# Two output blocks taken in turn: the order of the matmuls in a three-product fp32r trunk

## The chip, the cores and the metric

The kernel runs on one core of one Trainium2 chip. The metric is the device time of one launch in microseconds (us), median of three runs.

## The reference

The reference is a two-layer post-norm decoder trunk on x of 512 tokens by 1024 features, float32 throughout. Only the parts that matter here:

```
for i in range(2):
    x = layer_norm(ALPHA * x + 0.5 * swiglu(x, ffn1_w_gu[i], ffn1_w_down[i]), ...)
    if i == 0: y, qm = gla_mix(x @ gla_w_in, ...)      # gated linear attention
    else:      y, qm = conv_mix(x @ conv_w_in, ...)    # GLU, 31-tap depthwise convolution, layer norm
    m = mem_attention(qm, mem, mem_w_kv[i])            # 256 memory rows, 4 heads
    x = layer_norm(ALPHA * x + concatenate([y, m]) @ w_out, ...)
    x = layer_norm(ALPHA * x + 0.5 * swiglu(x, ffn2_w_gu[i], ffn2_w_down[i]), ...)

def swiglu(x, w_gu, w_down):                           # w_gu 1024 x 5632, w_down 2816 x 1024
    a, b = split(x @ w_gu, 2); return (silu(a) * b) @ w_down
```

## The kernel before

**Layout.** Activations are kept transposed: features on the 128 partitions, the 512 tokens along the free dimension, so x is eight blocks of 128x512. A PSUM bank holds one output block of 128x512 float32.

**Three products.** Every large product runs in the fp32r form of the matmul. A float32 operand is split into a rounded part (hi) and the remainder (lo), and a product is the sum of hi*hi, hi*lo and lo*hi (weights named first). `mm3` (L1228) issues these three, one after the other, into one bank: L1231 with weights whi and activations hi, L1232 with whi and lo, L1233 with wlo and hi. Every matmul comes with a weight load of its own.

**Weights.** They stream through in 206 chunks of up to eight k-blocks by 256 columns (two output blocks, called t = 0 and 1), in two slots. For each chunk SP loads it into `raw`, ACT rounds it into `whi` (`split_hi`, L479) once the slot is free (`w_used`), POOL (sometimes DVE) subtracts to make `wlo` (`split_lo`, L314, L870) and raises `lo_ready`, for which PE waits. Each engine's order is written out by hand; PE, ACT, DVE and POOL meet in semaphores only.

**The stages around the change.**
- `chunk` (L1235) is one chunk against x: k outside, t inside, so that the bank changes after every three matmuls. Used for the gate/up product of each of the four FFNs (22 chunks each; one bank pair for gate, one for up) and for the input projections. Two chunks of the GLA projection have one output block only, on bank 2 alone (`chunk(n0 + 1, 1, (2,))`, `chunk(n0 + 3, 1, (2,))`, L1485, L1492).
- `by_halves` (L1246) is the form of the first chunk after a layer norm, which follows x block by block as it becomes ready: per k two matmuls into the first bank, two into the second (L1253), then one each of the previous k's lo part (L1258).
- `down_pair` (L1275) is the FFN's second product: four pairs p of output blocks, each over 22 k-blocks in four chunks c of 6, 6, 6 and 4. Inside a chunk t is outside and k inside: all matmuls of t = 0 (bank 0), then all of t = 1 (bank 1). In the last chunk `y_even` is raised after t = 0, `w_used` after t = 1. Pairs 1 to 3 use the same two banks, and wait per bank for its evacuation (`y_evac`). Pairs 1 and 2 are a hardware loop on PE, ACT and DVE.
- `out_a` and `out_b` (L1350, L1362) are the output projections: over four k-blocks of the memory attention and eight of the mixer; t outside, k inside, two bank pairs. On PE the order is out_a(0), out_a(1), out_b(0), out_b(1), out_a(2), out_a(3), out_b(2), out_b(3), with a by_halves in place of out_b(0) after the convolution.
- `shift_sum` (L1299) stands on PE right behind pair 0 of each of these six products. It sums the first finished block over partitions and so waits for the first evacuation of the pair. `sums_u` (L1315) stands before the last k-block of pair 3.

**What follows a pair.** On DVE `residual_pair` (L911) takes, for t = 0: the residual (L923, and L927 in the output projections, L921 for the first block), the wait for `y_even`, the evacuation of bank t = 0 with the add (L934), the running sum (`add_sum`, L895; in pair 0 instead `take_shift`, L909); for t = 1: the running sum of squares of the block before (`add_square`, L903 or L900), the residual, the wait for `w_used`, the evacuation (L934), the sum, the square. On ACT `down_pair` (L514) has the splits of the coming chunks up to c = 0 of the next pair, then `squares` (L508) of both blocks, each after its evacuation, and only then the split of c = 1 of the next pair. In `out_proj` (L525) the split for slot 1 of out_a(3) stands behind the squares of pair 1, and that of the next stage's first chunk behind those of block 4 and 5.

Of the kernel before, what the change touches and what calls it, by code (L numbers as in the profile page):

```python
# [85 lines left out]
def build(nc, a, out):  # L86
    kv_dram = nc.dram_tensor("kv_scratch", (DEPTH, P, 2048), F32, kind="Internal").ap()
    with ExitStack() as ctx:
# [775 lines left out]
        def _(dve):  # L864
# [78 lines left out]
            def residual_ffn(ln, n0):  # L943
                residual_pair(ln, 0, n0 + 4, 0.5)
                with dve.Fori(1, 3) as p:
                    residual_pair(ln, p, n0 + 4 * p + 4, 0.5)
                residual_pair(ln, 3, n0 + 16, 0.5, last=True)
# [279 lines left out]
        def _(pe):  # L1227
# [6 lines left out]

            def chunk(n, s, banks, ready=None):  # L1235

                pe.wait_ge(lo_ready, n + 1)
                if ready is not None:
                    last = by_halves(s, banks, xhi, xlo, ready, True)
                else:  # L1240
                    for k in range(DK):
                        for t, b in enumerate(banks):
                            last = mm3(bank[b][:, :], s, k, t, xhi[:, k, :], xlo[:, k, :], k == 0, k == DK - 1)
                last.then_inc(w_used, 1)

            def by_halves(s, banks, hi, lo, ready, start):  # L1246

                for k in range(DK + 1):
                    if k < DK:
                        pe.wait_ge(x_hi_ready, ready + k + 1)  # L1250
                        for t, b in enumerate(banks):
                            for half in (whi, wlo):
                                nc.tensor.matmul(bank[b][:, :], half[:, s, k, t * P:t * P + P], hi[:, k, 0:SEQ],  # L1253
                                                 start=(start and k == 0 and half is whi), stop=False)
                    if k:
                        pe.wait_ge(x_ready, ready + k)
                        for t, b in enumerate(banks):
                            last = nc.tensor.matmul(bank[b][:, :], whi[:, s, k - 1, t * P:t * P + P], lo[:, k - 1, :],  # L1258
                                                    start=False, stop=(k == DK))
                            if k == DK and t == 0 and not start:  # L1260
                                last.then_inc(y_even, 1)
                return last
# [12 lines left out]
            def down_pair(f, p):  # L1275

                ln, n = LN_FFN[f], FFN_N[f] + FK + 4 * p
                first = isinstance(p, int)
                k0 = 0
                for c, kc in enumerate(DOWN_K):  # L1280
                    pe.wait_ge(lo_ready, n + c + 1)
                    if first and p == 0:
                        pe.wait_ge(h_done, FK * f + k0 + kc)
                        if c == 0:
                            pe.wait_ge(silu_done, FK * (f + 1))
                    for t in range(2):
                        if c == 0 and not (first and p == 0):
                            pe.wait_ge(y_evac, 8 * ln + 2 * p - 1 + t)
                        for k in range(k0, k0 + kc):
                            if first and p == 3 and t == 1 and k == FK - 1:  # L1290
                                sums_u(ln)
                            last = mm3(bank[t][:, :], c % 2, k - k0, t, h_hi[:, k, :], h_lo[:, k, :], k == 0, k == FK - 1)
                        if t == 1:
                            last.then_inc(w_used, 1)
                        elif c == len(DOWN_K) - 1:
                            last.then_inc(y_even, 1)
                    k0 += kc
# [41 lines left out]
            def ffn(f, between=None):  # L1339
# [5 lines left out]
                with pe.Fori(1, 3) as p:  # L1345
                    down_pair(f, p)
                down_pair(f, 3)
                stats(LN_FFN[f], (GLA_N, FFN_N[2], CONV_N, None)[f])

            def out_a(ln, n0, p, m, mo_hi, mo_lo):  # L1350
# [6 lines left out]
                for t in range(2):  # L1357
                    for k in range(A_K):
                        last = mm3(bank[b0 + t][:, :], p % 2, k, t, mo_hi[:, k, :], mo_lo[:, k, :], k == 0, False)
                last.then_inc(w_used, 1)  # L1360

            def out_b(ln, n0, p, y_h, y_l, base):  # L1362
# [3 lines left out]
                if p == 0 and base is not None:  # L1366
                    by_halves(0, (0, 1), y_h, y_l, base, False).then_inc(w_used, 1)
                    return
                for t in range(2):
                    for k in range(B_K):  # L1370
                        if p == 0 and t == 0:
                            pe.wait_ge(y_done, k + 1)
                        if p == 3 and t == 1 and k == B_K - 1:
                            sums_u(ln)
                        last = mm3(bank[b0 + t][:, :], p % 2, k, t, y_h[:, k, :], y_l[:, k, :], False, k == B_K - 1)
# [70 lines left out]
            for n in range(8):  # L1446
# [3 lines left out]
                for k in range(DK):  # L1450
                    if n == 0:
                        pe.wait_ge(mem_ready, k + 1)
                    for t in range(2):
                        last = mm3(bank[2 * (n % 2) + t][:, 0:NMEM], n % 2, k, t, mem_hi[:, k, :], mem_lo[:, k, :], k == 0, k == DK - 1)
# [157 lines left out]
            def diag_chunk(g):  # L1612
# [5 lines left out]
                for j in range(TAPS_K[g]):  # L1618
                    tap = 8 * g + j
                    for t in range(2):  # L1620
                        last = mm3(bank[2 + t][:, :], g % 2, j, t, cin_hi[:, t, tap:tap + SEQ], cin_lo[:, t, tap:tap + SEQ],
                                   tap == 0, tap == WIDTH - 1)
# [81 lines left out]
```

## Time and profile before

| | |
|---|---|
| median of 3 runs | 2279.32 us (2277.9 to 2279.92) |
| profiled execution, first to last instruction (span) | 2278.2 us |
| its mean granted TensorE clock | 0.967 |
| PE busy | 2163.0 us, 95% |
| PEld (weight loads) | 1748.7 us, 77% |
| POOL, DVE, ACT busy | 944.2, 830.9, 697.3 us |
| DMA | 195.62 MB, mean 86 GB/s |

The profiled execution comes with its span alone; no separate time of it is given, and the span is 1.1 us under the median. PE is TensorE's matmuls, PEld its weight loads (they run beside matmuls), DVE VectorE, ACT ScalarE, POOL GpSimd, SP SyncE. The durations of matmuls overlap, as a matmul starts before the one before has drained, so the pace is read from starts. A granted clock of 1.00 is 2.4 GHz, 0.50 is 1.2 GHz.

### The profile page before, as it was taken

The numbers are of one execution on the slowest core, as the hardware profiler recorded it, in microseconds if no ns is written. First come the engines' busy times: TensorE is split into PE (matmuls) and PEld (weight loads), VectorE is DVE, ScalarE is ACT, GpSimd is POOL, SyncE is SP. The second block draws the span as 40 slices with busy tenths as digits, with TensorE's granted clock in tenths as the row PEclk, the third lists the DMA queues.
The fourth block names the chain that finished last, engine by engine and source line by source line (L and its number), as shares of the span: only waits on it lengthen the run. The fifth ranks groups of instructions, "written<-read, shape, count | busy, mean of one in ns | idle before, by whom it ended". The sixth has DMA issues, their size and how long they took to land.

```text
span 2278.2 us, 24232 instructions
## 1 busy us (share of the span) xinstructions
PE 2163.0 (95%) x9608; PEld 1748.7 (77%) x9608; DVE 830.9 (36%) x963; ACT 697.3 (31%) x900; POOL 944.2 (41%) x295
## 2 busy tenths in 40 slices
PE   7999999999899999999999999998587899999998
PEld 7888888678777788887868888776465577888886
DVE  2233221424425432331142332125499753332213
ACT  5322222364313322222232222224145333222222
POOL 3244433443122444443344443436776234444342
PEclk9999999999989999999999999999798799999999
DMA  6422222232102223222322222232110122223221
GB/s 207 166 92 92 94 84 95 70 111 82 48 19 91 76 96 106 92 78 88 111 71 96 92 92 83 89 106 75 56 37 7 49 93 74 92 92 98 83 91 60
DMA packets 191706, 195.62 MB, mean 86 GB/s; under 512 B 3567, under 2 KB 190061, under 8 KB 191388
## 3 DMA queue, kind: packets, MB, share of 16 engines
q1 hardware_dynamic: 191036, 192.62, 26.0%
q10 hardware_dynamic: 608, 2.13, 0.2%
q8 instruction: 44, 0.72, 0.1%
q14 instruction: 18, 0.15, 0.0%
HBM read 190.54 MB, written 4.19 MB: 85 GB/s over the span
## 4 chain that ended last, share of the span: by engine, by line
PE 85%; DVE 5%; POOL 4%; ACT 3%; issue 1%; DMA 1%; DVEq 0%; POOLq 0%; ACTq 0%
PE bank L1231 26%; PE bank L1233 26%; PE bank L1232 26%; POOL wlo L314 3%; PE bank L1306 1%; DVE u L1173 1%; POOL xlo L324 1%; ACT u L543 1%; PE bank L1576 1%; ACT whi L479 1%; DMA raw<-in_mem_w_kv_dram 1%; PE bank L1332 1%; DVE scratch L895 1%; DVE scratch L956 0%; PE bank L1570 0%
## 5 line engine op out<-in xcount | busy, mean ns | idle before, releaser
L314 POOL TENSOR_TENSOR wlo<-raw,whi 128x2048 fp32r<-128x2048 f32 (+2 forms) x184 | 786.6, 4275 | 1155.9 <-ACT whi L479 1155.9
L1231 PE MATMUL bank<-xhi,whi 128*128 128x512 f32 x1712 | 673.4, 393 | 35.9 <-POOL wlo L314 35.9
L479 ACT CAST whi<-raw 128x2048 fp32r<-128x2048 f32 (+2 forms) x202 | 341.5, 1690 | 1194.4 <-PE bank L1233 1157.8
L1233 PE MATMUL bank<-xhi,wlo 128*128 128x512 f32 x1712 | 669.9, 391 | 0.0
L1232 PE MATMUL bank<-xlo,whi 128*128 128x512 f32 x1712 | 669.9, 391 | 0.0
L1231 PEld LDWEIGHTS bank<-xhi,whi 128*128 128x128 f32 x1712 | 323.6, 189 | 105.8 <-issue 37.8
L1233 PEld LDWEIGHTS bank<-xhi,wlo 128*128 128x128 f32 x1712 | 323.3, 189 | 67.7
L1232 PEld LDWEIGHTS bank<-xlo,whi 128*128 128x128 f32 x1712 | 323.7, 189 | 67.3 <-issue 0.5
L877 DVE TENSOR_TENSOR scratch<-scratch,bank 128x512 f32<-128x512 f32 x88 | 56.5, 684 | 631.5 <-PE bank L1233 631.5
L1231 PE MATMUL bank<-h_hi,whi 128*128 128x512 f32 x704 | 281.0, 399 | 0.1
L1233 PE MATMUL bank<-h_hi,wlo 128*128 128x512 f32 x704 | 278.5, 396 | 0.0
L1232 PE MATMUL bank<-h_lo,whi 128*128 128x512 f32 x704 | 278.5, 396 | 0.0
L880 DVE TENSOR_TENSOR h_lo<-scratch,h_hi 128x512 f32 (+1 forms) x88 | 223.3, 2575 | 53.2 <-ACT h_hi L496 53.2
L934 DVE SCALAR_TENSOR_TENSOR u<-bank,u 128x512 f32<-128x512 f32 (+1 forms) x48 | 33.2, 691 | 404.9 <-PE bank L1233 403.4
L1231 PEld LDWEIGHTS bank<-h_hi,whi 128*128 128x128 f32 x704 | 132.5, 188 | 34.7 <-POOL wlo L314 1.9
L1232 PEld LDWEIGHTS bank<-h_lo,whi 128*128 128x128 f32 x704 | 132.5, 188 | 32.0 <-issue 1.0
L1233 PEld LDWEIGHTS bank<-h_hi,wlo 128*128 128x128 f32 x704 | 132.5, 188 | 32.0
L1173 DVE SCALAR_TENSOR_TENSOR u<-conv_in,w_dw,u 128x512 f32<-128x512 f32 x170 | 131.1, 843 | 0.0
L324 POOL TENSOR_TENSOR xlo<-u,xhi 128x512 fp32r<-128x512 f32 x48 | 70.0, 1477 | 48.0 <-ACT u L543 28.9
L508 ACT ACTIVATE scratch<-u 128x512 f32<-128x512 f32 (+1 forms) x56 | 35.1, 632 | 154.0 <-DVE u L934 136.2
L870 DVE TENSOR_TENSOR wlo<-raw,whi 128x2048 fp32r<-128x2048 f32 (+1 forms) x18 | 40.7, 2262 | 58.2 <-ACT whi L479 58.2
L496 ACT CAST h_hi<-scratch 128x512 f32 (+1 forms) x88 | 49.9, 615 | 0.0
(235 smaller groups left out, 1913.8 us busy)
## 6 DMA issues: line engine op xcount, KB each, us to landing
raw<-in_ffn_w_gu_dram SPq DMA_DIRECT2D x88, 1024.0 KB, 5.0
raw<-in_ffn_w_down_dram SPq DMA_DIRECT2D x48, 768.0 KB, 4.4
raw<-in_gla_w_in_dram SPq DMA_DIRECT2D x13, 1024.0 KB, 5.3
raw<-in_conv_w_in_dram SPq DMA_DIRECT2D x10, 1024.0 KB, 5.0
raw<-in_mem_w_kv_dram SPq DMA_DIRECT2D x8, 1024.0 KB, 6.6
raw<-in_ffn_w_down_dram SPq DMA_DIRECT2D x16, 512.0 KB, 3.4
raw<-in_gla_w_out_dram SPq DMA_DIRECT2D x4, 1024.0 KB, 5.2
raw<-in_conv_w_out_dram SPq DMA_DIRECT2D x4, 1024.0 KB, 5.1
```

The costliest lines, as they stand in the source:

```text
L314: nc.gpsimd.tensor_tensor(wlo[:, s, 0:kc, 0:width], raw[:, s, 0:kc, 0:width], whi[:, s, 0:kc, 0:width].bitcast(F32), ALU.subtract).then_in ...
L324: nc.gpsimd.tensor_tensor(lo[:, k, :], u[:, k, :], hi[:, k, 0:SEQ].bitcast(F32), ALU.subtract).then_inc(x_ready, 1)
L479: nc.scalar.copy(whi[:, s, 0:kc, 0:width], raw[:, s, 0:kc, 0:width]).then_inc(hi_ready, 1)
L496: nc.scalar.copy(h_hi[:, bass.ds(2 * i + t, 1), :], act_out[t].rearrange("p (a s) -> p a s", a=1)).then_inc(h_hi_done, 1)
L508: nc.scalar.activation(sq[t], u[:, bass.ds(d, 1), :].rearrange("p a s -> p (a s)"), ACT.Square).then_inc(sq_done, 1)
L870: nc.vector.tensor_tensor(wlo[:, s, 0:kc, 0:width], raw[:, s, 0:kc, 0:width], whi[:, s, 0:kc, 0:width].bitcast(F32), ALU.subtract).then_in ...
L877: nc.vector.tensor_tensor(act_out[t], act_out[t], bank[2 + t][:, :], ALU.mult).then_inc(mul_done, 1)
L880: nc.vector.tensor_tensor(h_lo[:, bass.ds(2 * i + t, 1), :], act_out[t].rearrange("p (a s) -> p a s", a=1), h_hi[:, bass.ds(2 * i + t, 1), ...
L1173: nc.vector.scalar_tensor_tensor(out=u[:, c, :], in0=src, scalar=w, in1=u[:, c, :], op0=ALU.mult, op1=ALU.add).then_inc(taps_done, 1)
L1231: nc.tensor.matmul(to, whi[:, s, k, w], hi, start=start, stop=False)
L1232: nc.tensor.matmul(to, whi[:, s, k, w], lo, start=False, stop=False)
L1233: return nc.tensor.matmul(to, wlo[:, s, k, w], hi, start=False, stop=stop)
```

## The change

Where `mm3` gave all three products of one output block, a new helper gives each product for both blocks before the next product, so that consecutive matmuls write two banks in turn. Chunks, the memory keys' projection, the convolution's taps and the out and down products use it; `by_halves` turns its two inner loops round. The four down pairs use banks 0, 1 and 2, 3 alternately (`b0 = 2 * (p % 2)`), wait for the evacuation of the pair before the last one only, and are unrolled on PE and DVE. In pair 3 the last chunk of `down_pair`, and the last four k-blocks of `out_b`, keep t outside and the order of `mm3`. The number of matmuls and of weight loads is the same.

```diff
 def residual_ffn(ln, n0):
-    residual_pair(ln, 0, n0 + 4, 0.5)
-    with dve.Fori(1, 3) as p:
-        residual_pair(ln, p, n0 + 4 * p + 4, 0.5)
-    residual_pair(ln, 3, n0 + 16, 0.5, last=True)
+    for p in range(4):
+        residual_pair(ln, p, n0 + 4 * p + 4, 0.5, b0=2 * (p % 2), last=p == 3)
...
+def mm3_in_turn(tos, s, k, his, los, start, stop):
+    for n, (half, xs) in enumerate(((whi, his), (whi, los), (wlo, his))):
+        last = [nc.tensor.matmul(to, half[:, s, k, t * P:t * P + P], xs[t], start=(start and n == 0),
+                                 stop=(stop and n == 2)) for t, to in enumerate(tos)]
+    return last
...
 def chunk(n, s, banks, ready=None):
         for k in range(DK):
-            for t, b in enumerate(banks):
-                last = mm3(bank[b][:, :], s, k, t, xhi[:, k, :], xlo[:, k, :], k == 0, k == DK - 1)
+            last = mm3_in_turn([bank[b][:, :] for b in banks], s, k, [xhi[:, k, :]] * 2, [xlo[:, k, :]] * 2,
+                               k == 0, k == DK - 1)[-1]
...
 def by_halves(s, banks, hi, lo, ready, start):
-            for t, b in enumerate(banks):
-                for half in (whi, wlo):
+            for half in (whi, wlo):
+                for t, b in enumerate(banks):
...
 def down_pair(f, p):
-    ln, n = LN_FFN[f], FFN_N[f] + FK + 4 * p
-    first = isinstance(p, int)
+    ln, n, b0 = LN_FFN[f], FFN_N[f] + FK + 4 * p, 2 * (p % 2)
+    to = [bank[b0][:, :], bank[b0 + 1][:, :]]
     for c, kc in enumerate(DOWN_K):
...
-        for t in range(2):
-            if c == 0 and not (first and p == 0):
-                pe.wait_ge(y_evac, 8 * ln + 2 * p - 1 + t)
+        elif p >= 2 and c == 0:
+            pe.wait_ge(y_evac, 8 * ln + 2 * (p - 2) + 2)
+        if p == 3 and c == len(DOWN_K) - 1:
+            for t in range(2):
+                for k in range(k0, k0 + kc):
+                    if t == 1 and k == FK - 1:
+                        sums_u(ln)
+                    last = mm3(to[t], c % 2, k - k0, t, h_hi[:, k, :], h_lo[:, k, :], False, k == FK - 1)
+                last.then_inc(w_used if t else y_even, 1)
+        else:
             for k in range(k0, k0 + kc):
-                if first and p == 3 and t == 1 and k == FK - 1:
-                    sums_u(ln)
-                last = mm3(bank[t][:, :], c % 2, k - k0, t, h_hi[:, k, :], h_lo[:, k, :], k == 0, k == FK - 1)
-            if t == 1:
-                last.then_inc(w_used, 1)
-            elif c == len(DOWN_K) - 1:
-                last.then_inc(y_even, 1)
+                even, last = mm3_in_turn(to, c % 2, k - k0, [h_hi[:, k, :]] * 2, [h_lo[:, k, :]] * 2,
+                                         k == 0, k == FK - 1)
+            if c == len(DOWN_K) - 1:
+                even.then_inc(y_even, 1)
+            last.then_inc(w_used, 1)
...
 def ffn(f, between=None):
-    with pe.Fori(1, 3) as p:
+    for p in range(1, 4):
         down_pair(f, p)
-    down_pair(f, 3)
...
 def out_a(ln, n0, p, m, mo_hi, mo_lo):
-    for t in range(2):
-        for k in range(A_K):
-            last = mm3(bank[b0 + t][:, :], p % 2, k, t, mo_hi[:, k, :], mo_lo[:, k, :], k == 0, False)
+    for k in range(A_K):
+        last = mm3_in_turn([bank[b0][:, :], bank[b0 + 1][:, :]], p % 2, k, [mo_hi[:, k, :]] * 2,
+                           [mo_lo[:, k, :]] * 2, k == 0, False)[-1]
...
 def out_b(ln, n0, p, y_h, y_l, base):
+    to = [bank[b0][:, :], bank[b0 + 1][:, :]]
+    together = B_K - 4 if p == 3 else B_K
+    for k in range(together):
+        if p == 0:
+            pe.wait_ge(y_done, k + 1)
+        even, last = mm3_in_turn(to, p % 2, k, [y_h[:, k, :]] * 2, [y_l[:, k, :]] * 2, False, k == B_K - 1)
+    if p < 3:
+        even.then_inc(y_even, 1)
+        last.then_inc(w_used, 1)
+        return
     for t in range(2):
-        for k in range(B_K):
-            if p == 0 and t == 0:
-                pe.wait_ge(y_done, k + 1)
-            if p == 3 and t == 1 and k == B_K - 1:
+        for k in range(together, B_K):
+            if t == 1 and k == B_K - 1:
                 sums_u(ln)
-            last = mm3(bank[b0 + t][:, :], p % 2, k, t, y_h[:, k, :], y_l[:, k, :], False, k == B_K - 1)
+            last = mm3(to[t], p % 2, k, t, y_h[:, k, :], y_l[:, k, :], False, k == B_K - 1)
         last.then_inc(w_used if t else y_even, 1)
```

The products of the memory keys and of the convolution's taps change in the same way as `out_a`.

## Rows read from the trace of the kernel before

**Rows 1.** The page: the chain that ended last, shares of the span by engine
```profile
PE 85%; DVE 5%; POOL 4%; ACT 3%; issue 1%; DMA 1%; DVEq 0%; POOLq 0%; ACTq 0%
```

**Rows 2.** Windows, PE alone: stretch, its us, PE busy (x matmuls touched), granted clock, DMA
```profile
100.00:300.00 200.00, 200.00 (x884) 1.00 0.29 96
350.00:430.00 80.00, 80.00 (x345) 1.00 0.30 92
```

**Rows 3.** Timeline of PE, one-bank chunk, first and last of 18 (start, duration, us)
```profile
477.29 0.39 PE L1231 MATMUL bank<-xhi,whi 128*128 128x512 f32 x1
...
481.14 0.39 PE L1233 MATMUL bank<-xhi,wlo 128*128 128x512 f32 x1
```

**Rows 4.** Timeline of PE, by_halves of the first FFN: 18 matmuls from first to last start
```profile
69.71 0.39 PE L1253 MATMUL bank<-xhi,whi 128*128 128x512 f32 x1
...
73.79 0.39 PE L1253 MATMUL bank<-xhi,whi 128*128 128x512 f32 x1
```

**Rows 5.** Timeline of PE, first FFN: last even matmul of pair 1, first of pair 2's c = 0 and 1
```profile
368.30 0.40 PE L1233 MATMUL bank<-h_hi,wlo 128*128 128x512 f32 x1
...
371.34 0.40 PE L1231 MATMUL bank<-h_hi,whi 128*128 128x512 f32 x1
...
379.73 0.39 PE L1231 MATMUL bank<-h_hi,whi 128*128 128x512 f32 x1
```

**Rows 6.** Timeline of DVE at that boundary
```profile
368.74 0.69 DVE L934 SCALAR_TENSOR_TENSOR u<-bank,u 128x512 f32 x1 [23.59 <-PE bank L1233]
...
372.96 0.69 DVE L934 SCALAR_TENSOR_TENSOR u<-bank,u 128x512 f32 x1
```

**Rows 7.** Timeline of ACT and of POOL at that boundary
```profile
373.78 0.64 ACT L508 ACTIVATE scratch<-u 128x512 f32 x1 [3.52 <-DVE u L934]
374.32 1.47 ACT L479 CAST whi<-raw 128x1536 fp32r<-128x1536 f32 x1
...
367.57 3.50 POOL L314 TENSOR_TENSOR wlo<-raw,whi 128x1536 fp32r<-128x1536 f32 x1 [6.51 <-ACT whi L479]
375.87 3.50 POOL L314 TENSOR_TENSOR wlo<-raw,whi 128x1536 fp32r<-128x1536 f32 x1 [4.79 <-ACT whi L479]
```

**Rows 8.** Timeline of DVE, GLA output projection, pair 1: the steps without a loop
```profile
729.03 0.69 DVE L895 TENSOR_TENSOR scratch<-scratch,u 128x512 f32<-128x512 f32 x1
729.69 0.69 DVE L903 TENSOR_TENSOR scratch<-scratch 128x512 f32<-128x512 f32 x1
730.30 0.68 DVE L923 SCALAR_TENSOR_TENSOR u<-xlo,scratch 128x512 f32<-128x512 f32 x1
731.02 0.69 DVE L927 SCALAR_TENSOR_TENSOR u<-xhi,u 128x512 f32<-128x512 f32 x1
731.75 0.69 DVE L934 SCALAR_TENSOR_TENSOR u<-bank,u 128x512 f32<-128x512 f32 x1
```

**Rows 9.** Timeline of PE: a shift sum that waited; and a half-clock stretch, its first matmul and the first past it
```profile
1830.83 1.13 PE L1301 MATMUL bank<-u,ones 128*128 128x512 f32 x2 [0.74 <-DVE u L934]
...
1620.64 0.77 PE L1231 MATMUL bank<-xhi,whi 128*128 128x512 f32 x1 [28.63 <-POOL wlo L314]
...
1625.32 0.39 PE L1233 MATMUL bank<-xhi,wlo 128*128 128x512 f32 x1
```

**Rows 10.** Timeline of ACT, POOL and PE, GLA output: out_a(2) to out_a(3)
```profile
733.01 1.04 ACT L479 CAST whi<-raw 128x1024 fp32r<-128x1024 f32 x1
...
734.12 2.39 POOL L314 TENSOR_TENSOR wlo<-raw,whi 128x1024 fp32r<-128x1024 f32 x1 [6.40 <-ACT whi L479]
...
736.61 0.46 PE L1231 MATMUL bank<-mo_hi_g,whi 128*128 128x512 f32 x1
```

**Rows 11.** Timeline of POOL, DVE and PE, GLA output, out_b(3): to sums_u
```profile
756.97 4.65 POOL L314 TENSOR_TENSOR wlo<-raw,whi 128x2048 fp32r<-128x2048 f32 x1 [7.83 <-ACT whi L479]
...
760.07 2.11 DVE L895 TENSOR_TENSOR scratch<-scratch,u 128x512 f32<-128x512 f32 x1
...
763.97 0.50 PE L1306 MATMUL bank<-ones,scratch 128*128 128x1 f32 x4
```

More of the change, by code:

```diff
@@ L1281, in down_pair @@
                     pe.wait_ge(lo_ready, n + c + 1)
-                    if first and p == 0:
+                    if p == 0:
                         pe.wait_ge(h_done, FK * f + k0 + kc)
@@ L1368, in out_b @@
                     return
+                to = [bank[b0][:, :], bank[b0 + 1][:, :]]
+                together = B_K - 4 if p == 3 else B_K
+                for k in range(together):
+                    if p == 0:
+                        pe.wait_ge(y_done, k + 1)
[4 more added lines that the diff above has]
+                    return
                 for t in range(2):
-                    for k in range(B_K):
-                        if p == 0 and t == 0:
-                            pe.wait_ge(y_done, k + 1)
-                        if p == 3 and t == 1 and k == B_K - 1:
+                    for k in range(together, B_K):
+                        if t == 1 and k == B_K - 1:
                             sums_u(ln)
-                        last = mm3(bank[b0 + t][:, :], p % 2, k, t, y_h[:, k, :], y_l[:, k, :], False, k == B_K - 1)
+                        last = mm3(to[t], p % 2, k, t, y_h[:, k, :], y_l[:, k, :], False, k == B_K - 1)
                     last.then_inc(w_used if t else y_even, 1)
@@ L1452, in _ @@
                         pe.wait_ge(mem_ready, k + 1)
-                    for t in range(2):
-                        last = mm3(bank[2 * (n % 2) + t][:, 0:NMEM], n % 2, k, t, mem_hi[:, k, :], mem_lo[:, k, :], k == 0, k == DK - 1)
+                    last = mm3_in_turn([bank[2 * (n % 2) + t][:, 0:NMEM] for t in range(2)], n % 2, k, [mem_hi[:, k, :]] * 2,
+                                       [mem_lo[:, k, :]] * 2, k == 0, k == DK - 1)[-1]
                 last.then_inc(w_used, 1)
@@ L1619, in diag_chunk @@
                     tap = 8 * g + j
-                    for t in range(2):
-                        last = mm3(bank[2 + t][:, :], g % 2, j, t, cin_hi[:, t, tap:tap + SEQ], cin_lo[:, t, tap:tap + SEQ],
-                                   tap == 0, tap == WIDTH - 1)
+                    last = mm3_in_turn([bank[2][:, :], bank[3][:, :]], g % 2, j, [cin_hi[:, t, tap:tap + SEQ] for t in range(2)],
+                                       [cin_lo[:, t, tap:tap + SEQ] for t in range(2)], tap == 0, tap == WIDTH - 1)[-1]
                 last.then_inc(w_used, 1)
```

## The prediction

> **What bounds the kernel now.** The chain that ended last comes first: 85% of the span on PE [rows 1]. So what matters is the pace of PE's matmuls and the places where PE waits. The exception is the convolution, where PE waits for POOL (28.63 us before one matmul [rows 9]) and a faster PE would bring little.
>
> The pace comes from windows. Between 100 and 300 us PE never rests, and 884 matmuls touch the 200 us; less the two at the ends that makes 0.2268 us each. In the down product it is 80 / 343 = 0.2332 us [rows 2]. At the granted clock of 1.00 (2.4 GHz) 512 columns pass in 0.2133 us, so 6% and 9% are lost inside the stream. The change is about that loss, if the loss comes from the bank.
>
> **Does the bank set the pace?** The kernel has three mixtures of bank changes on the same operands. In `chunk` one succession in three changes the bank: 0.2268 us. In the one-bank GLA chunk none does: 18 matmuls, 17 steps in 3.85 us, 0.2265 us [rows 3]. In `by_halves` four of six do, three of them in a row: 18 steps in 4.08 us, 0.2267 us [rows 4]. None, a third and two thirds of changes give the same pace to 0.1%. The slower down product repeats one bank, but so does the one-bank chunk, which is fast; what differs there is the activations (h in place of x), which the change does not move. I therefore take the changes of pace at nothing, for 7,248 matmuls of 512 columns. Bounds: if full alternation does what two thirds do not, each falls to 0.2133 us (the second rival); the products on h could fall to 0.2267, or pick up a further 0.007 us.
>
> The Trainium skill says the same of the mechanism: in "TensorE: Matmul & The Clock Gate", Step-by-step, the next matmul's fill overlaps the drain of the last, with no word of the bank, and its Back-to-back issue gap has 216 ns for 512 columns. The rows are 5 to 8% over that figure with and without a bank change; if the change closed that gap, the result would lie near the second rival's.
>
> **What the rotation of the down pairs saves.** In pairs 1 to 3 PE asks for the evacuation of the bank that it is about to fill. Where pair 2 begins PE goes on without a gap: the 13 steps from 368.30 to 371.34 us take 3.04 us, or 0.234 each [rows 5]. Nothing saved. Unrolling saves nothing either, as these steps go across a turn of the loop.
>
> **What the turn order costs.** In the old order block t = 0 of a pair is done a stretch of matmuls before t = 1: 12 in the FFN, 24 in `out_b`, some 2.8 and 5.6 us. DVE and ACT use them. In turn, t = 0 is done one matmul before t = 1, and their work comes in one piece behind the pair. ACT's order then matters: the split of the next pair's chunk c = 1 is queued behind the squares of both blocks, so behind both evacuations.
>
> *FFN, entry of pairs 2 and 3.* Let E be the start of the next pair, 371.34 [rows 5]. Now the odd evacuation starts at E + 1.62 [rows 6], the square 0.82 later, the split 0.54 later, POOL 1.55 later, for 3.50 [rows 7]: wlo is there at E + 8.03. PE needs it at 379.73 = E + 8.39 [rows 5]. There is only 0.36 us of slack. After the change the even evacuation starts 0.44 after its last matmul starts (368.74 less 368.30) [rows 5, 6], which now is two steps before E: E - 0.03. Then, by the steps of the code without a loop: evacuation to sum 0.73, sum to square's sum 0.66, to residual 0.61, to odd evacuation 0.72 [rows 8]. That is E + 2.69. ACT's square follows one such step later, then 0.54 + 1.55 + 3.50 as before: E + 9.01, and 0.05 to PE. PE waits 0.67 us, and 0.1 us more for the first matmul after a wait. Two entries in four FFNs: 8 x 0.75 = **6.0 us**. With loop steps (0.82 and 0.81) it would be 1.1 each; if a hand-over is hidden, 0.4. Pair 1 is not hit this way: its chain begins with the shift sum, and PE itself moves with that.
>
> *Shift sum.* It stands on PE between pairs 0 and 1 and needs the even evacuation. In old order that is long done. In turn it ends 0.44 + 0.69 after the start of the second-last matmul, and PE goes 0.05 later: 0.95 us after the last matmul's start, not 0.23. The trace has this case once, where the convolution's out_b(0) already ends with one matmul per block: idle 0.74 us [rows 9]. With the slow restart 0.8 us, for four FFNs and the GLA output: **4.0 us** (3.5 to 4.5). `by_halves` is no later than now.
>
> *out_a(3), both output projections.* Its split is queued behind the squares of pair 1. E1, out_a(2)'s start, is 24 steps before 736.61, so 731.01 [rows 10]. Now the odd evacuation is at E1 + 0.74 [rows 8] and PE finds wlo just in time (0.06 late). In turn: -0.03 + 0.73 + 0.66 + 0.61 + 0.72 + 0.73 (two residual steps here) = E1 + 3.42; square 0.73, split 0.54 as above, POOL 1.11 later for 2.39 [rows 10]: E1 + 8.19, where 5.60 is wanted. **2.6 us**, twice: 5.3 us (4.4 to 6.0).
>
> *The last pair of the output projections.* PE begins out_b(3) at about T = 753.5. The even block is done at its 36th matmul: evacuation at T + 8.6, sum at T + 9.3. POOL's split for the next stage, queued behind ACT's squares of block 5, moves from T + 3.5 to about T + 6.6 and lasts to T + 11.3. The sum cannot pass it: now it starts at 760.07, takes 2.11 us in place of 0.69, and ends 0.56 us after POOL does at 761.62 [rows 11]. So it ends near T + 11.85; PE wants it at 763.97, T + 10.5. That is 1.4 us, and as the odd block's residual comes behind it, some 0.3 more before the statistics: 1.7 us, twice, **3.4 us** (0 to 5). The Trainium skill has this block as a rule ("SBUF — State Buffer", Who interferes with whom: VectorE with two SBUF inputs and GpSimd lock each other out for a whole instruction); the row agrees. Pair 3 of the FFNs keeps its order in its last chunk, and its tail stays.
>
> **Sum.** 6.0 + 4.0 + 5.3 + 3.4 = 18.7 us on the profiled span of 2278.2: 2296.9. The median of the runs is 1.1 us above that span: **2298 us**, 0.8% slower. By the bounds of the four terms 2290 to 2304. A measurement of this kernel tells about 0.2%, 4.6 us, from no change.
>
> **Rivals.**
> 1. *The down pace recovers.* The activations' order changes (hi, hi, lo, lo, hi, hi), and the 2,112 matmuls on h with some 400 of the output products run at 0.2267 us: -16.7 us, with 2 us more waiting as chunk c = 0 is shorter. 2298 - 15 = 2283 us. For: the pace differs between operands, so something about their reads counts. Against: x has the same pace in three orders. Chance 0.11.
> 2. *The bank is the bound after all* (the other side). Only a stream that never repeats a bank escapes. It decides from some 2.7 ns a matmul, as 7,000 x 2.7 ns pays the 19 us. At 0.2133 us: 4,650 matmuls on x outside the convolution x 13.4 ns = 62 us, 2,112 x 20 = 42, output products 10; less 28 us of waits, which grow with PE's speed: 2193 us; half of it 2245. For: no stream of the trace alternates throughout. Against: [rows 2 to 4]. Chance 0.15.
> 3. *The waits are hidden*: DVE and ACT hand over faster than the added steps, only the shift sums cost: 2283 us. Chance 0.07.
> 4. *The clock falls at the new waits.* After a wait of 28.63 us the matmuls ran at half clock (1.2 GHz) from 1620.64 to 1625.32, 11 of them, 2.2 us lost [rows 9]. At 15 new waits that is 33 us: 2331. Against: the new waits are under 3 us. The Trainium skill has a rule that speaks against the change ("TensorE: Matmul & The Clock Gate", A second HAM failure mode: cycling through PSUM banks leaves small idle times at which the clock oscillates). `by_halves` changes banks at full pace [rows 4], so the trace does not bear it out. Chance 0.05.
>
> That the change does not do what it says is no case: the program's order is PE's order.
>
> **How the numbers follow.** My forecast has 0.62. Its own range is 2290 to 2304. With rivals 1 and 3 (2283) and room for a half-clock stretch after the longest waits the range is 2277 to 2310; rivals 2 and 4, 0.20, are left out. Faster by over 0.2%: rival 2 and the better end of rival 1, 0.18. Within 0.2%: the rest of rival 1 and rival 3, 0.12. Slower: 0.70.
>
> **What would show it.** Windows over x chunks: 0.2267 us a matmul again, and 0.233 on h; 0.22 or less proves me wrong. PE's waits should list the shift sum behind DVE's L934 five times at some 0.7 us, and behind POOL's wlo a wait of some 0.7 us at c = 1 of pairs 2 and 3 of each FFN and of 2.6 us at each out_a(3). ACT's second square of a pair should start 2 us later against the pair's end. If these waits are there and the time is still lower, the pace fell.

## The result, and the profile after

The changed kernel takes 2310.0 us (median of four runs, 2300.71 to 2314.03), the kernel before 2279.6 beside it: ratio 1.0119, 95% interval 1.0101 to 1.0136. It is slower, by 30.4 us in these runs. Four further runs in another batch (e5 below) gave 2308.8 us against 2283.4, ratio 1.0118 (1.0098 to 1.0138), so 25 to 30 us is the cost to explain. The profiled execution spans 2298.6 us, 20.4 over the one before, and is the fastest of the four.

The page, the chain that ended last by engine (before: [rows 1]):

```profile
PE 63%; issue 16%; POOL 11%; DVE 5%; ACT 4%; DMA 1%; POOLq 0%; DVEq 0%; ACTq 0%
```

POOL's share has risen from 4 to 11%. "issue" is time for which the profile shows no wait; PE and issue are 79% together, 86% before.

Windows of PE over the matmuls on x, then over those on h (stretch, its us, PE busy with the matmuls touched, granted clock, DMA):

```profile
100.00:300.00 200.00, 200.00 (x884) 1.00 0.29 96
350.00:430.00 80.00, 78.36 (x334) 1.00 0.30 92
```

On x the count is the same 884. In the down product 11 fewer are in the window, as it holds the entries of pairs 2 and 3: PE is idle for 1.64 us there, and the first step after each wait is slow. From start to start at full clock, leaving out steps that hold a wait, a matmul takes 0.2269 us on x and 0.2333 on h on average, in both kernels. **The stream is not faster by a nanosecond.** What is new are waits. PE's waits (us in total, times, longest):

```profile
PE bank L1236 <- POOL wlo L314: 49.5, 14, 28.6
...
PE bank L1316 <- DVE scratch L895: 7.3, 4, 2.3
...
PE bank L1311 <- DVE u L934: 3.8, 6, 0.7
```

The same three in the kernel before:

```profile
PE bank L1231 <- POOL wlo L314: 37.8, 4, 28.6
...
PE bank L1306 <- DVE scratch L895: 4.6, 2, 2.3
...
PE bank L1301 <- DVE u L934: 0.7, 1, 0.7
```

So ten waits for POOL's `wlo` are new, two for the sums (DVE's `add_sum`) and five for the shift sum: the numbers of places that the prediction named.

**One entry of a pair.** The timeline where pair 2 of the first FFN begins answers to [rows 5 to 7]. PE:

```profile
380.31 0.63 PE L1236 MATMUL bank<-h_hi,wlo 128*128 128x512 f32 x2
381.76 0.73 PE L1236 MATMUL bank<-h_hi,whi 128*128 128x512 f32 x2 [0.82 <-POOL wlo L314]
382.32 0.63 PE L1236 MATMUL bank<-h_lo,whi 128*128 128x512 f32 x2
```

DVE:

```profile
372.42 0.69 DVE L934 SCALAR_TENSOR_TENSOR u<-bank,u 128x512 f32<-128x512 f32 x1 [26.22 <-PE bank L1236]
373.14 0.69 DVE L895 TENSOR_TENSOR scratch<-scratch,u 128x512 f32<-128x512 f32 x1
373.98 0.69 DVE L903 TENSOR_TENSOR scratch<-scratch 128x512 f32<-128x512 f32 x1
...
375.31 0.69 DVE L934 SCALAR_TENSOR_TENSOR u<-bank,u 128x512 f32<-128x512 f32 x1
```

ACT, then POOL:

```profile
373.31 0.64 ACT L508 ACTIVATE scratch<-u 128x512 f32 x1 [4.78 <-DVE u L934]
376.13 0.63 ACT L508 ACTIVATE scratch<-u 128x512 f32 x1 [2.18 <-DVE u L934]
376.67 1.47 ACT L479 CAST whi<-raw 128x1536 fp32r<-128x1536 f32 x1
```

```profile
378.22 3.49 POOL L314 TENSOR_TENSOR wlo<-raw,whi 128x1536 fp32r<-128x1536 f32 x1 [6.11 <-ACT whi L479]
```

Pair 2 begins at E = 372.38; behind the 36 matmuls of its chunk c = 0 the next would start at 380.78. The odd evacuation starts at E + 2.93, the second square at E + 3.75, the split at E + 4.29, and POOL ends at E + 9.33. PE starts at 381.76 in place of 380.78: 0.98 us late, and its first step takes 0.34 in place of 0.23, so some 1.08 us are lost; the other seven entries lose 1.07 to 1.09. The chain is the one predicted, step for step; it ends 0.32 us later than the predicted E + 9.01. DVE's step from sum to square's sum is 0.84 us, not 0.66, as L903 needs ACT's square of the even block, which began 0.89 us after its evacuation and ended at 373.95. ACT's `down_pair` still runs as a hardware loop for pairs 1 and 2; in the GLA output, without a loop, the same step of ACT is 0.73.

**The shift sum.** PE at the end of pair 0:

```profile
340.32 1.12 PE L1311 MATMUL bank<-u,ones 128*128 128x512 f32 x2 [0.62 <-DVE u L934]
```

PE waits 0.62 us for the evacuated block that the sum reads, and as long at the other three FFNs and in the GLA output.

**out_a(3) of the GLA output** ([rows 10]), ACT, POOL and then PE:

```profile
733.44 0.63 ACT L508 ACTIVATE scratch<-u 128x512 f32<-128x512 f32 x1 [2.81 <-DVE u L934]
733.98 2.95 ACT L479 CAST whi<-raw 128x1024 fp32r<-128x1024 f32 x2
```

```profile
735.09 2.35 POOL L314 TENSOR_TENSOR wlo<-raw,whi 128x1024 fp32r<-128x1024 f32 x1 [9.16 <-ACT whi L479]
```

```profile
737.49 1.22 PE L1236 MATMUL bank<-mo_hi_g,whi 128*128 128x512 f32 x2 [2.50 <-POOL wlo L314]
738.51 1.05 PE L1236 MATMUL bank<-mo_lo_g,whi 128*128 128x512 f32 x2
739.37 1.05 PE L1236 MATMUL bank<-mo_hi_g,wlo 128*128 128x512 f32 x2
740.22 0.87 PE L1236 MATMUL bank<-mo_hi_g,whi 128*128 128x512 f32 x2
740.92 0.62 PE L1236 MATMUL bank<-mo_lo_g,whi 128*128 128x512 f32 x2
741.39 0.39 PE L1236 MATMUL bank<-mo_hi_g,wlo 128*128 128x512 f32 x1
```

PE waits 2.50 us, and then ten matmuls take 3.90 us (737.49 to 741.39) in place of 10 x 0.2333. So this wait costs 2.50 + 1.57 = 4.1 us: the granted clock fell to half (1.2 GHz) as the wait ended. Windows of all engines (PE, PEld, DVE, ACT, POOL busy, then clock and DMA), the GLA attention stage and this place, in the changed kernel and then in the kernel before:

```profile
630.00:650.00 20.00, 17.08 (x99) 14.45 (x99) 4.60 (x9) 3.25 (x6) 0.00 (x0) 0.91 0.00 1
736.00:742.00 6.00, 4.51 (x13) 3.61 (x14) 3.59 (x3) 0.93 (x1) 1.44 (x1) 0.72 0.58 190
```

```profile
630.00:650.00 20.00, 18.94 (x79) 16.76 (x80) 3.04 (x6) 2.17 (x4) 0.00 (x0) 0.66 0.00 1
736.00:742.00 6.00, 6.00 (x27) 4.74 (x26) 3.21 (x3) 1.91 (x1) 0.51 (x1) 1.00 0.53 176
```

The first window works the other way. There the kernel before had a clock of 0.66 (13.7 us at half clock) and this execution 0.91 (3.4 us): 10.3 us less at half clock, half of it lost time where PE is the bound, so up to 5 us of luck. The second execution of the changed kernel had the full 13.7 us (e5). So the profiled span shows only 20.4 us of the cost: outside the stages of the table further down this execution is 4.3 us shorter than the one before, e5's only 0.3.

**The last pair of the GLA output** ([rows 11]), POOL, DVE and PE:

```profile
762.57 4.62 POOL L314 TENSOR_TENSOR wlo<-raw,whi 128x2048 fp32r<-128x2048 f32 x1 [11.06 <-ACT whi L479]
```

```profile
764.52 0.69 DVE L934 SCALAR_TENSOR_TENSOR u<-bank,u 128x512 f32<-128x512 f32 x1 [1.77 <-PE bank L1231]
765.25 2.50 DVE L895 TENSOR_TENSOR scratch<-scratch,u 128x512 f32<-128x512 f32 x1
```

```profile
766.12 0.40 PE L1231 MATMUL bank<-y_hi,wlo 128*128 128x512 f32 x1
767.80 1.05 PE L1316 MATMUL bank<-ones,scratch 128*128 128x1 f32 x8 [1.28 <-DVE scratch L895]
768.71 0.48 PE L1229 MATMUL bank<-y_hi,whi 128*128 128x512 f32 x1
```

The sum takes 2.50 us in place of 0.69 and ends 0.56 us behind POOL, as before. PE's step over the sums is 2.59 us (766.12 to 768.71). In the kernel before it was 1.04:

```profile
763.74 0.40 PE L1233 MATMUL bank<-y_hi,wlo 128*128 128x512 f32 x1
...
764.78 0.48 PE L1231 MATMUL bank<-y_hi,whi 128*128 128x512 f32 x1
```

That is 1.55 us more.

### The profile page after: what moved, and what is told of

Its sections match the earlier page's. It is cut to its first block, busy times and chain, and to the rows that moved or that the text cites. A ratio compares the mean times of both kernels' runs of the same rounds, so it can differ in the third digit from the quotient of the medians.

```text
span 2298.6 us, 24106 instructions
## 1 busy us (share of the span) xinstructions
PE 2168.2 (94%) x9608; PEld 1744.9 (76%) x9608; DVE 821.1 (36%) x963; ACT 697.9 (30%) x900; POOL 944.6 (41%) x295
## 4 chain that ended last, share of the span: by engine, by line
PE 63%; issue 16%; POOL 11%; DVE 5%; ACT 4%; DMA 1%; POOLq 0%; DVEq 0%; ACTq 0%
PE bank L1236 56%; POOL wlo L314 9%; PE bank L1316 1%; DVE u L1171 1%; POOL xlo L324 1%; ACT whi L479 1%; ACT u L543 1%; DVE scratch L895 1%; DMA raw<-in_mem_w_kv_dram 1%; PE bank L1342 1%; PE bank L1593 1%; PE bank L1344 1%; DVE scratch L954 0%; PE bank L1323 0%; PE bank L1229 0%
## 5 line engine op out<-in xcount | busy, mean ns | idle before, releaser
L1236 PE MATMUL bank<-xhi,whi 128*128 128x512 f32 x1712 | 533.6, 392 | 36.0 <-POOL wlo L314 36.0
L1236 PE MATMUL bank<-xlo,whi 128*128 128x512 f32 x1712 | 530.4, 390 | 0.0
L1236 PE MATMUL bank<-xhi,wlo 128*128 128x512 f32 x1712 | 529.6, 390 | 0.0
L1236 PE MATMUL bank<-h_hi,whi 128*128 128x512 f32 x672 | 214.0, 399 | 6.8 <-POOL wlo L314 6.6
L1236 PE MATMUL bank<-h_lo,whi 128*128 128x512 f32 x672 | 211.2, 395 | 0.0
L1236 PE MATMUL bank<-h_hi,wlo 128*128 128x512 f32 x672 | 211.1, 395 | 0.0
L934 DVE SCALAR_TENSOR_TENSOR u<-bank,u 128x512 f32<-128x512 f32 x48 | 33.2, 692 | 454.3 <-PE bank L1236 351.2
L1236 PEld LDWEIGHTS bank<-h_hi,whi 128*128 128x128 f32 x672 | 125.2, 188 | 43.0 <-POOL wlo L314 12.0
L1236 PEld LDWEIGHTS bank<-h_hi,wlo 128*128 128x128 f32 x672 | 126.2, 188 | 30.6
L1236 PEld LDWEIGHTS bank<-h_lo,whi 128*128 128x128 f32 x672 | 126.2, 188 | 30.5
```

Source lines behind the costliest of these rows:

```text
L934: nc.vector.scalar_tensor_tensor(out=blk(u, d), in0=bank[b0 + t][:, :], scalar=coef, in1=blk(u, d), op0=ALU.mult, op1=ALU.add).then_inc(y_ ...
L1236: last = [nc.tensor.matmul(to, half[:, s, k, t * P:t * P + P], xs[t], start=(start and n == 0), stop=(stop and n == 2)) for t, to in enume ...
```

## The experiments

Each ratio is to the kernel before in the same batch of runs. None of these kernels leaves anything out; all run the 9608 matmuls of the program.

**e1: the kernel before, with one block after the other in `chunk`**, so that the bank repeats for 24 matmuls.

```diff
-                    for k in range(DK):
-                        for t, b in enumerate(banks):
+                    for t, b in enumerate(banks):
+                        for k in range(DK):
```

> The kernel before, with chunk's loops turned the other way: all matmuls of block 0, then all of block 1, so that the bank of the x products changes once in 24 matmuls in place of once in three. If the bank of the matmul before plays no part (my theory), x chunks run at 0.2267 us a matmul again and the time is that of before, 2280 us within 3. If repeating a bank costs anything (rival), it is more here: a third of some 4,650 successions repeats more often; at the 20 ns by which the pace misses 512 columns in the down product that is 31 us, 2311 us.

Measured: 2281.34 us, ratio 1.0004 (0.9994 to 1.0013), 0.2269 us a matmul on x. From no change of bank to a change each time, the pace on x is the same; the bank has no part in it.

**e2: the changed kernel, with the old order in the last chunk of every down pair and in `out_b`.** Only the first four k-blocks of out_b(3) stay in turn, as in the changed kernel. The turn order of the rest, the other banks and the unrolling stay.

```diff
-                    if p == 3 and c == len(DOWN_K) - 1:
+                    if c == len(DOWN_K) - 1:
...
-                together = B_K - 4 if p == 3 else B_K
+                together = B_K - 4 if p == 3 else 0
...
```

> The changed kernel, but every pair ends as pair 3 of the FFNs does: the last chunk of down_pair with t outside, and out_b with t outside throughout (out_b(3) keeps its first four k-blocks in turn). Bank rotation, unrolling and the turn order of everything else stay. If the late even block is the cause (my theory), the five waits of the shift sum and the waits at c = 1 and at out_a(3) are gone: 2281 us, at most 2284 with the rest in out_b(3). If the turn order itself is slow, or the rotation or the unrolled code (rivals), it stays at 2300 to 2310.

Measured: 2282.15 us, ratio 1.0001 (0.9988 to 1.0014). PE's waits:

```profile
PE bank L1236 <- POOL wlo L314: 37.9, 4, 28.6
...
PE bank L1316 <- DVE scratch L895: 4.6, 2, 2.3
...
PE bank L1311 <- DVE u L934: 0.7, 1, 0.7
```

All three are back at the counts of before, and so is the time. The whole cost lies in the late even block; rotation, unrolling and the order inside the other chunks together cost and bring nothing, to some 3 us (the interval).

**e3: the changed kernel, with ACT's split of the next pair's c = 1 (and of out_a(3)) ahead of both squares.**

```diff
-                squares(LN_FFN[f], p)
+                if last:
+                    squares(LN_FFN[f], p)
                 split_hi(t0 + 2, 1, 8 if last else DOWN_K[1], P if last and f == 0 else 256, late=f == 3)
+                if not last:
+                    squares(LN_FFN[f], p)
...
+                    if q == 0:
+                        split_hi(t0 + 2, 1, A_K)
                     squares(ln, 2 * q + 1)
-                    split_hi(t0 + 2, 1, A_K if q == 0 else 8)
+                    if q:
+                        split_hi(t0 + 2, 1, 8)
```

> The changed kernel, with ACT's order changed alone: the split of the next pair's c = 1 (pairs 0 to 2), and that of out_a(3), stand before the squares of the pair in place of behind them. By my theory the waits at c = 1 of pairs 2 and 3 and at out_a(3) are gone (some 11.5 us with the clock's share), and the shift sums (4 us) and the last pair of the output projections (3 us) stay: 2288 to 2295 us. The small wait at c = 1 of pair 1, which the kernel before has too, goes as well. If the waits come from POOL or the loads and not from ACT's order, nothing changes: 2300 to 2310.

Measured: 2296.3 us, ratio 1.0055 (1.0038 to 1.0073): 15 us over the kernel before, where the changed kernel has 25 to 30. PE's waits for `wlo` are at the old level, those of the sums (here L1322) and of the shift sum (L1317) stay:

```profile
PE bank L1242 <- POOL wlo L314: 37.8, 4, 28.6
...
PE bank L1322 <- DVE scratch L901: 7.3, 4, 2.3
...
PE bank L1317 <- DVE u L940: 3.9, 6, 0.8
```

At each out_a(3) a wait of 0.7 us behind an evacuation (L1242 behind L940) has come in place of the one for `wlo`. The terms "entry of pairs 2 and 3" and "out_a(3)", 11.3 us in the prediction, are shown in their mechanism: the split queued behind the squares.

**e4: the kernel before, with 64 more bytes a partition ahead of the area that h, y and the mixers' tensors share.**

```diff
-        small = sb("small", [P, 16])
+        small = sb("small", [P, 32])
```

> The kernel before, with one small tensor 64 bytes longer, which moves h, y, c and the attention's outputs by 64 bytes in each partition; x and the weights stay. If the slower pace of the down product (0.2333 us against 0.2267) comes from where its activations lie against a 128-byte line (one theory), h runs at 0.2267 us and the time falls by 14 to 17 us to some 2264. If it comes from the repeated bank, from the operands' number or order, nothing changes: 2280 us.

Measured: 2267.56 us, ratio 0.9934 (0.9917 to 0.995): **faster than both kernels**. The mean on h, y and mo_g falls from 0.2333 to 0.2270 us; the down stages take 122.2, 125.0, 125.2 and 122.3 us in place of 125.0, 127.6, 128.2 and 125.0. The window on h:

```profile
350.00:430.00 80.00, 80.00 (x352) 1.00 0.30 92
```

345 were there before. So a part of the loss that the change aimed at lay in where the activations lie.

**e5: the changed kernel once more.**

> The changed kernel, nothing altered, for a second profiled execution and more times: the first profiled one was 2300.7 us and the median of four 2310.0. The waits are set by the program and should be the same to 0.1 us: by them 2298 to 2302. If the rest of the median comes from the clock (my theory now), a slower execution shows more half-clock time in the GLA attention stage and behind the waits at out_a(3), and the stages between keep their lengths. If it comes from longer waits or a slower pace (rival), these show in the rows.

Measured: 2308.8 us, ratio 1.0118 (1.0098 to 1.0138); profiled span 2304.8. Its trace shows what the first one hid. PE at the end of the GLA output projection:

```profile
773.98 0.39 PE L1231 MATMUL bank<-y_hi,wlo 128*128 128x512 f32 x1
775.68 1.05 PE L1316 MATMUL bank<-ones,scratch 128*128 128x1 f32 x8 [1.30 <-DVE scratch L895]
776.59 0.53 PE L1229 MATMUL bank<-y_hi,whi 128*128 128x512 f32 x1
...
777.35 0.63 PE L1231 MATMUL bank<-y_hi,wlo 128*128 128x512 f32 x1
```

The wait for the sums is the same 1.3 us as in the first trace, but here the clock falls behind it: matmuls of 0.63 us. It stays at half for 13.7 us, over the statistics and into the next FFN. The window from there (PE busy, clock):

```profile
771.00:811.00 40.00, 36.20 (x136) 0.83 0.17 53
```

**e6: the changed kernel, with all of `out_b` in the old order**: the lines of e2 on `out_b`, but with `together = 0` for out_b(3) too. The down pairs stay as changed.

> The changed kernel with out_b's old order (t outside) for all four pairs; down_pair, out_a, chunks and bank rotation as changed. By my theory the output projections give back 6.6 and 5.1 us (their lengths 76.1 and 99.0 us fall to some 69.5 and 93), with the half-clock stretches behind the out_a(3) waits, and the FFNs keep their 12: 2292 to 2297. If the cost were in the FFNs alone it stays at 2305 or more; if the waits at out_a(3) cost most, it falls below 2290.

Measured: 2293.74 us, ratio 1.0048 (1.0031 to 1.0064). The output stages are back at 69.5 and 93.5 us, the down stages stay at 128.0, 130.6, 130.6 and 128.0. PE has 12 waits for `wlo` (44.3 us), eight more than before: those of the down pairs. So the two output projections are worth 15 us, more than the 9.5 predicted for them and more than the 9.6 to 11.7 by which their own stages had grown. The window that answers to e5's:

```profile
771.00:811.00 40.00, 37.27 (x153) 0.91 0.20 68
```

**e7 and e8: e4's edit with 192 and with 128 bytes**, one run each.

> The kernel before with h, y, c and the attention's outputs moved by 192 bytes in place of 64: h then begins at a multiple of 256 bytes, x and the weights at 128 over one. If a 128-byte line counts alone, h runs at 0.2267 us as with 64 bytes (span near 2268). If h must lie as the weights do, at 128 over a multiple of 256, it stays at 0.2333 (span near 2280).

> The same with 128 bytes: h begins 64 bytes over a 128-byte line again, as in the kernel before. By either reading of the alignment h runs at 0.2333 us, span near 2280; 0.2267 us here would say that the 64-byte result was not of alignment.

Measured: 2284.3 us with 192 bytes, h at 0.2328; 2270.35 us with 128 bytes, h at 0.2291. The second contradicts what I had expected of it, so both readings of the alignment were wrong.

**e9: 64 bytes ahead of everything**, x and the weights moved with h.

```diff
+        sb("ahead", [P, 16])
         xhi = sb("xhi", [P, DK, SEQ], F32R)
```

> The kernel before, with 64 unused bytes a partition ahead of everything, so that x, the weights and the shared area (h) all move by 64 bytes. In e4 only the shared area moved, by the same 64 bytes, and h fell from 0.2333 to 0.2270 us a matmul. If the activations' own address sets the pace, h is at 0.227 again, and x, which moves for the first time, may leave its 0.2269: I expect 0.2269 to 0.233. If what counts is how h lies against the weights, h is back at 0.2333 here, x unchanged, and the time is 2280 us.

Measured, in one run: 2282.24 us, x at 0.2269, h back at 0.2333:

```profile
350.00:430.00 80.00, 80.00 (x345) 1.00 0.30 92
```

So it is not h's own address. What e4 changed was the distance of h from what did not move with it.

**e10: the changed kernel with e4's 64 bytes.**

> The changed kernel with the 64 bytes of e4 ahead of the shared area. My theory has pace and order apart: h at 0.227 us again, and the cost of the order the same or a little larger, as chunk c = 0 is 36 x 0.0063 = 0.23 us shorter for each late split. So 2267.6 + 27 to 30 = 2295 to 2299 us, ratio to the kernel before 1.007. If the order and the slow pace of h had to do with each other, the change would cost some 10 us less or more here than it does without the 64 bytes.

Measured: 2296.21 us, ratio 1.0062 (1.0043 to 1.008), h at 0.2269. Set against e4, each by its own kernel before, the change costs 28 us, as it costs 25 to 30 without the bytes. Its down stages sum to 508.3 us against 494.7 in e4, 13.6 more, where the change had cost 11.9 without the 64 bytes: the 8 x 0.23 us of a shorter c = 0. Here the pace on h and the order act apart from each other.

**e11: the changed kernel, pair 0 in the old order** (last chunk of every FFN's pair 0, out_b(0) of the GLA output).

```diff
-                    if p == 3 and c == len(DOWN_K) - 1:
+                    if p in (0, 3) and c == len(DOWN_K) - 1:
...
-                together = B_K - 4 if p == 3 else B_K
+                together = B_K - 4 if p == 3 else 0 if p == 0 else B_K
...
```

> The changed kernel with the last chunk of pair 0 of every FFN, and out_b(0) of the GLA output, in the old order: the block that the shift sum needs is done a stretch earlier, and the shift sum's wait goes, as in the kernel before. By the prediction's term 0.8 x 5 = 4.0 us: 2305 us. Each FFN's down stage should fall from 128.1, 131.0, 130.6, 128.0 us by 0.7 to 0.9, the GLA output stage by as much, the convolution's not at all. The rival: the shift sum's wait hides others of PE behind it, and then the stages stay.

Measured: 2303.65 us, ratio 1.0099 (1.0083 to 1.0116): 21.9 us over the kernel before of its batch, 3.5 less than e5. The shift sum's wait is gone:

```profile
PE bank L1236 <- POOL wlo L314: 49.4, 14, 28.6
...
PE bank L1311 <- DVE u L934: 0.7, 1, 0.7
```

The down stages fall by 0.9, 0.2, 0.9 and 0.9 us against the changed kernel's trace, the GLA output by 0.6: 3.5 in all, where 4.0 was predicted. The intervals of e11's and e5's ratios overlap, so it is the gone waits and the stages that show this, not the times.

**e12: the kernel before with e4's bytes, 64 more in front of the convolution's later tensors, and the split of c = 1 between the two squares.**

```diff
-        small = sb("small", [P, 16])
+        small = sb("small", [P, 32])
...
-            ("conv_in", [P, DK, PAD + SEQ], F32), ("qm_c", [P, HEADS, SEQ], F32),
+            ("conv_in", [P, DK, PAD + SEQ], F32), ("gap", [P, 16], F32), ("qm_c", [P, HEADS, SEQ], F32),
...
-                squares(LN_FFN[f], p)
+                if last:
+                    squares(LN_FFN[f], p)
+                else:
+                    squares(LN_FFN[f], p, only=0)
                 split_hi(t0 + 2, 1, 8 if last else DOWN_K[1], P if last and f == 0 else 256, late=f == 3)
+                if not last:
+                    squares(LN_FFN[f], p, only=1)
...
```

> The kernel before in its own order, with e4's 64 bytes, 64 more bytes ahead of the convolution's later tensors, and the split of the next pair's c = 1 on ACT between the two squares of a pair. What e4 to e9 have in common is the distance of the activations from the weights whi, modulo 256 bytes: x has 0 and 0.2269 us; h has 192, 0, 64 and 128 with 0, 64, 128 and 192 bytes, and 0.2333, 0.2270, 0.2291, 0.2328; mo_c has 128, 192, 0, 64 and 0.2327, 0.2333, 0.2278, 0.2292. If that is the rule, here all have 0, and mo_c and c, at 0.2333 and 0.2294 in e4, come to 0.227 to 0.228: some 1 us less. The rival, that only an absolute address counts, leaves them at 0.2291 or above. The split takes away PE's five short waits at c = 1 that e4 added (38.9 us in 9 waits for wlo L314, back to 37.8 in 4): 1 us. Together 2265.5 us, 0.993 of the kernel before, the fastest so far by little.

Measured: 2266.93 us, ratio 0.9939 (0.9924 to 0.9954). Every tensor that is split into hi and lo now lies at distance 0 from the weights (modulo 256 bytes; the last section has the table), and mo_c comes to 0.2272, c to 0.2274, as the distance rule had it, against 0.2333 and 0.2294 in e4. On h:

```profile
350.00:430.00 80.00, 80.00 (x353) 1.00 0.29 92
```

The waits for `wlo`, 38.9 us in 9 in e4, where a shorter c = 0 had brought five small ones, are back at 37.9 us in 4. The split stands there for pairs 0 to 2 and for pair 1 of the output projections. In time e12 can't be told from e4; both beat both kernels.

## Why the prediction was right, and where its sizes were off

The direction, the places and the kind of wait came as forecast. The size did not: 2310.0 us is the very top of the range of 2277 to 2310 and outside the forecast's own 2290 to 2304, and the 30.4 us are 1.6 times the 18.7 of the sum. That the range held the median is partly luck, as its top came from "room for a half-clock stretch" and no term of the sum. Which terms were too small stands under 3, 5 and 6.

Lengths in us, from the profiled executions: the four down stages and the two output stages (first to last start of their matmuls), and the two entries behind the output projections (from their last matmul to the 101st on x after it).

| | before | after | e5 | e11 | e3 | e6 | e2 |
|---|---|---|---|---|---|---|---|
| down stages, sum | 505.8 | 517.7 | 517.3 | 514.8 | 508.5 | 517.2 | 507.4 |
| output stages, sum | 163.4 | 175.1 | 173.0 | 174.8 | 169.2 | 163.0 | 162.6 |
| entries, sum | 71.9 | 73.0 | 77.7 | 75.4 | 76.2 | 71.8 | 70.2 |
| the three, more than before | | 24.7 | 26.9 | 23.9 | 12.8 | 10.9 | -0.9 |
| median, more than before | | 30.4 | 25.4 | 21.9 | 15.3 | 10.3 | 1.1 |

The last two rows agree to 2.5 us but for the first trace, whose runs spread over 13 us. To that the cost is accounted for.

1. **Bank and pace: right.** A bank change at every step gives the 0.2269 us of none. Rival 2 is out (the changed kernel, e1), and rival 1 too, as h keeps 0.2333 in the new order. Against the change the Trainium skill ("TensorE: Matmul & The Clock Gate", A second HAM failure mode) tells of a bf16 kernel in which cycling through PSUM banks brought small idle times and an oscillating clock. This trace does not show that: the window over 200 us of strict alternation has no idle time and a clock of 1.00. Where half-clock time came anew, the idle time ahead of it was from the late block (points 5 and 6), not from the bank.
2. **Rotation and unrolling: right at nothing**, to some 3 us (e2).
3. **Entry of pairs 2 and 3, 6.0 us: right place, too small.** It measured 1.08 us in the entry read above, 8 x 1.08 = 8.6, where the prediction had 0.75 each. The step that failed is the chain "by the steps of the code without a loop", which had DVE from sum to square's sum in 0.66 us. It took 0.84, as the square's sum needs ACT's square, and ACT, whose code still is a loop there, began it 0.89 us after the evacuation. At pair 3 of the same FFN, which stands outside ACT's loop, the square begins 0.73 us after the evacuation (433.61 to 434.34) and DVE's step is 0.67, the prediction's value to 0.01. No run unrolled ACT.
4. **Shift sums, 4.0 us: right**, 3.5 us in the stages of e11. Its cost against e5's (21.9 for 25.4) says the same, within the noise.
5. **out_a(3), 5.3 us: the wait right, the term too small.** The wait is 2.50 us as predicted (2.6), but a half-clock stretch behind it adds 1.57: 8.2 us for two. Rival 4 put this at 2.2 us for each new wait and held against it that they were under 3 us. For the long ones that did not help: of the ten waits for `wlo` the two of 2.5 us drew one (in the first trace and e5, at both places), the eight of 0.8 us none.
6. **Last pair of the output projections, 3.4 us: right in its stage, incomplete beyond.** PE's step grew by 1.55 us, twice 3.1; the 0.3 us for the odd block was not told apart. What its sum left out is the clock: in the five profiles of kernels with out_b(2) in turn, the half-clock time at the ten entries is 6.8 us three times and 10.2 to 13.4 seven times; in the nine others it is never over 6.8. An entry took 36.5 to 38.9 us in the five and 34.7 to 36.6 in the nine. This is up to 6 us for two, and e6's 15 us hold it. It is out_b(2) that counts and not the order of out_b(3) itself: e2 is one of the nine and has out_b(3) as the changed kernel has it. There POOL's split starts 3.50 us after out_b(3) begins, as in the kernel before, and the sum takes 0.69 us; in the changed kernel it starts 6.72 us after (the prediction had 6.6). What moves it is the square of block 5, the odd block of pair 2.

By terms: FFNs 11.9 us in place of 9.2, output projections 11.7 in place of 9.5, entries 1.1 to 5.8 in place of nothing, so 25 to 27 against 18.7. The rest of the miss (30.4 in the first batch) is not tied to a place; the kernel before had medians from 2279.6 to 2283.5 in five batches, so some of it is how the runs fall. Rival 3 (waits hidden) is out: DVE and ACT hand over no faster than the steps that the prediction took. What decides whether a wait of 1.3 us draws a half-clock stretch (e5) or not (the first trace) stays open.

## What to carry to other kernels

Before an order inside a pair of blocks is changed for the sake of the matmul stream, look for a place in the trace where the stream already runs both ways, and then cost what follows the block: a block that ends earlier than its partner is cover for the evacuation, the squares and every split queued behind them. Here that cover was worth the whole 25 to 30 us, and the order inside the stream nothing. Put work that PE waits for ahead of work that nobody waits for in an engine's queue; e3 got back 10 us or more by that alone. If matmuls of one shape run at different paces on different tensors, compare the tensors' addresses against the weights' before the order.

## What the hardware showed that I had not expected

**The pace depends on the distance between activations and weights in SBUF, modulo 256 bytes.** By the program's allocation (in order, each tensor rounded up to 32 bytes) `whi` begins at byte 82,048 of a partition, `xhi` at 16,512, `h_hi` at 136,768, `mo_hi_c` at 162,304; whi and wlo, and the hi and lo parts of each of these, have the same remainder. Microseconds a matmul of 512 columns at full clock:

| distance mod 256 | 0 | 64 | 128 | 192 |
|---|---|---|---|---|
| x (before, e9) | 0.2269 | | | |
| h (e4, e8, e7, before) | 0.2270 | 0.2291 | 0.2328 | 0.2333 |
| mo_c (e8, e7, before, e4) | 0.2278 | 0.2292 | 0.2327 | 0.2333 |
| mo_c, c (e12) | 0.2272, 0.2274 | | | |

e9 shows that the distance counts and not h's own address; the columns were read off e4 to e8, and e12 was their forecast. Two tensors agree column by column. The distance is called one from the weights because a matmul on h reads nothing else; x, `u`, `raw` and `scratch` have the weights' remainder in every one of these kernels, so no run separates them. The table holds for multiples of 64 bytes: the convolution's taps, whose activations begin 4 bytes further on with each tap, take 0.2325 to 0.2335 us on average in all of these kernels, also in e12, where they run through the distances 0 to 120 in steps of 4. That was not followed up. Products on c, whose hi and lo parts lay at different distances (192 and 128) before e12, ran at 0.2302 to 0.2331 with no simple place in the table. Why the distance counts, perhaps as reads of a matmul's activations beside the next weight load, was not tried. The gain in this kernel is 0.6%, for 64 unused bytes.
